# Gate weights by one rounded matmul per token, and all first products before the second ones

## What is computed

```python
idx = jnp.take_along_axis(cand_idx, pos, axis=-1)
g = jax.nn.softmax(top_s, axis=-1).astype(h.dtype)
...
def block(args):
    xt, it, gt = args
    u = expert_u[it]
    act = jax.nn.gelu(jnp.einsum('td,tkd->tk', xt, u))
    return jnp.einsum('tk,tkd->td', gt * act, expert_v[it])
```

## Time and profile before

| | us |
|---|---|
| median of three runs | 1509.1 (1508.21 to 1510.73) |
| the profiled execution, its time | 1509.89 |
| its span, first to last instruction | 1508.1 |
| TensorE busy | 1470.0 |
| VectorE busy | 889.2 |
| ScalarE busy | 819.0 |
| GpSimd busy | 576.4 |

### The profile page before, as it was taken

How to read it: one execution, slowest core, us unless ns; L and a number is a source line. 1 busy time by engine, 2 the same in 40 slices (tenths; PEclk the granted TensorE clock), 3 DMA queues, 4 the chain that set the end, 5 groups by cost and what they waited for, 6 DMA issues and landing times.

```text
span 1508.1 us, 24377 instructions
## 1 busy us (share of the span) xinstructions
PE 1470.0 (97%) x8923; PEld 1302.1 (86%) x8923; DVE 889.2 (59%) x2185; ACT 819.0 (54%) x1483; POOL 576.4 (38%) x200
## 2 busy tenths in 40 slices
PE   7999999999999999989999999999999999999998
PEld 6788888788889898889999998888888888887886
DVE  4935259388336431225996662666666666667776
ACT  5556454488456644443556664555555555555554
POOL 6881665700467477456888884000000000000000
PEclk9999999999999999999999999999999999999999
DMA  8740435600334335333665334555555555556774
GB/s 332 274 169 29 167 129 177 225 30 2 108 121 163 140 141 183 121 143 113 197 211 153 98 105 161 196 195 194 185 185 189 193 195 195 186 189 219 243 241 163
DMA packets 60125, 251.08 MB, mean 166 GB/s; under 512 B 6144, under 2 KB 18560, under 8 KB 44160
## 3 DMA queue, kind: packets, MB, share of 16 engines
q1 hardware_dynamic: 60032, 249.86, 47.9%
HBM read 242.50 MB, written 7.34 MB: 166 GB/s over the span
## 4 chain that ended last, share of the span: by engine, by line
PE 66%; POOL 2%; ACT 2%; DVE 1%; issue 1%; DMA 0%; DVEq 0%; ACTq 0%
PE bank L1297 23%; PE bank L1321 9%; PE bank L702 6%; PE bank L869 6%; PE bank L1324 5%; PE bank L1250 4%; PE bank L705 3%; POOL wlo L1364 2%; PE bank L822 2%; PE bank L764 1%; PE bank L805 1%; ACT whi L1421 1%; PE bank L724 1%; PE bank L998 1%; PE bank L1150 1%; PE bank L980 1%
## 5 line engine op out<-in xcount | busy, mean ns | idle before, releaser
L1364 POOL TENSOR_TENSOR wlo<-raw,whi 128x2048 fp32r<-128x2048 f32 (+1 forms) x51 | 195.3, 3840 | 159.0 <-ACT whi L1421 158.7
L1364 POOL TENSOR_TENSOR wlo<-arena,whi 128x2048 fp32r<-128x2048 f32 (+1 forms) x45 | 195.1, 4342 | 151.1 <-ACT whi L1421 150.9
L1297 PE MATMUL bank<-whi,ghi 128*128 128x512 f32 x512 | 201.4, 393 | 3.6 <-DVE glo L2559 1.7
L1297 PE MATMUL bank<-wlo,ghi 128*128 128x512 f32 x512 | 201.0, 393 | 0.0
L1297 PE MATMUL bank<-whi,glo 128*128 128x512 f32 x512 | 200.0, 391 | 0.0
L1321 PE MATMUL bank<-hT,whi 128*128 128x512 f32 x624 | 154.3, 390 | 1.6 <-ACT whi L1767 1.6
L1321 PEld LDWEIGHTS bank<-hT,whi 128*128 128x128 f32 x624 | 117.0, 188 | 26.0 <-ACT whi L1767 1.8
L2516 DVE TENSOR_TENSOR wlo<-raw,whi 128x1024 fp32r<-128x1024 f32 x84 | 102.8, 1225 | 56.6 <-ACT whi L1774 56.6
L1377 POOL TENSOR_TENSOR wlo<-raw,whi 128x1024 fp32r<-128x1024 f32 x52 | 123.8, 2391 | 28.2 <-ACT whi L1717 28.1
L1421 ACT ACTIVATE whi<-arena 128x2048 fp32r<-128x2048 f32 x41 | 78.4, 1915 | 94.4 <-PE bank L822 28.7
L822 PE MATMUL bank<-whi,hT 128*128 128x512 f32 x512 | 125.8, 393 | 0.0
(11 more groups left out here) (336 smaller groups left out, 3027.0 us busy)
## 6 DMA issues: line engine op xcount, KB each, us to landing
raw<-ex_in SPq DMA_DIRECT2D x52, 1024.0 KB, 4.8
raw<-w_in SPq DMA_DIRECT2D x44, 1024.0 KB, 5.2
arena<-w_in SPq DMA_DIRECT2D x44, 1024.0 KB, 5.1
raw<-ex_in SPq DMA_DIRECT2D x84, 512.0 KB, 3.9
xw<-ex_in SPq DMA_DIRECT2D x26, 1024.0 KB, 4.7
xw<-ex_in SPq DMA_DIRECT2D x16, 512.0 KB, 4.0
arena<-spill SPq DMA_DIRECT2D x48, 128.0 KB, 3.8
spill<-gact SPq DMA_DIRECT2D x32, 128.0 KB, 3.7
```

Of the source, the lines that this page charges most:

```text
L1297: last = mm(bank[2 * t + h][:, :], g[:, j % 2, tok], w[:, b, at], start=False, stop=(final and i == 2), skip_group_check=True)
L1364: last = G.tensor_tensor(wlo[:, u % 2, at], slots[u % RING][:, at], whi[:, u % 2, at], ALU.subtract)
```

## The change

All 128 first products are now taken in one stage, tiles 0 to 127, and all activations go to DRAM; then come all 128 second products, like the tail before. A *unit* is the `expert_u` half of a tile (n below 128) or the `expert_v` half (n from 128): `unit_hi`, `unit_lo`. Tiles 31 to 127 are merged.

W is built from tile 31 on: in each round of three tiles (n = 31 + 3g) one group g of eight tokens, in four *quarters* of two tokens, two behind the round's first tile and two behind its second. The gate values are themselves split in a rounded value and a remainder. One matmul of rounded operands with 256 columns gives a token's product with the rounded gate values and with their remainders (`hot_quarter`). ScalarE copies the one half to W, VectorE adds the other (`add_low`). For a group VectorE makes `plain` (1024 elements), from which GpSimd multiplies with the rounded gates (twice 512) and VectorE with the remainders (twice 512), and VectorE compares for the other side (twice 512; these four are `hots`). `iota8` is now read from SBUF. From tile 34 on every third remainder of the first products is made on VectorE.

In the second stage the activation m is read back (`load_act`) behind the load of unit m + 129.

```diff
+MERGED = 31
 GROUPS_W = T // 8
...
+NU = 2 * N_KEYS
+RING_OF = [n % 4 if n < G0 - 5 else n % 3 for n in range(NU)]
+LAST_OF_FOUR = max(n for n in range(NU) if RING_OF[n] == 3)
+BY_DVE = [n >= 2 * N_KEYS - 128 or (n > HOT0 and n % 3 == HOT0 % 3) for n in range(NU)]
...
+def quarters_at(i):
+    g, at = divmod(i - HOT0, 3)
+    return range(4 * g + 2 * at, 4 * g + 2 * at + 2) if 0 <= g < GROUPS_W and at < 2 else range(0)
...
+        plain_hot = quarters[3].rearrange("p (j n) -> p j n", j=8)
+        gated = [w[3].rearrange("p (a j n) -> p a j n", a=2, j=4) for w in (hi4, lo4)]
+        second_hot = [w[:, :, :].rearrange("p a t -> p (a t)").rearrange("p (j n) -> p j n", j=4) for w in (ghi, glo)]
+        staged = [gact[:, 0], gact[:, 1], xw[:, 4 * T:5 * T]]
+        again = [xw[:, T * (5 + i):T * (6 + i)] for i in range(3)]
...
+            def load_act(m):
+                if m >= 3:
+                    sp_.wait_ge(g_ready, m - 2)
+                sp_.wait_ge(act_stored[m % 3], 16 * (m // 3 + 1))
+                sp_.dma_start(again[m % 3], spill[m]).then_inc(act_back[m % 3], 16)
...
+                    by_dve, by_pool = lows_upto(earlier(n))
+                    if BY_DVE[earlier(n)]:
+                        sp_.wait_ge(u_lo_dve, by_dve)
+                    else:
+                        sp_.wait_ge(u_lo_pool, by_pool)
+                sp_.dma_start(quarters[RING_OF[n]], ex_d[n][:, 0:D] if n < N_KEYS else ex_d[n - N_KEYS][:, D:2 * D])\
+                   .then_inc(u_loaded[RING_OF[n]], 16)
+                if 6 <= n < N_KEYS + 6:
+                    store_act(n - 6)
+                m = n - 1 - N_KEYS
+                if m >= 0:
+                    load_act(m)
+            load_act(N_KEYS - 1)
...
+            def first_product(i):
+                h, l = (w[RING_OF[i]].rearrange("p (k n) -> p k n", k=KT) for w in (hi4, lo4))
+                else:
+                    pe.wait_ge(act_ready, i - 1)
+                if i == G0:
+                pe.wait_ge(u_hi, i + 1)
+                both = first_bank(i)[:, :].rearrange("p (s t) -> p s t", s=2)
+                out = both[:, 0 if i < MERGED else 1]
+                for k in range(KT):
+                    if i >= MERGED:
+                        mm(both, h[:, k, :], hT2[:, :, k, :], start=(k == 0), stop=False)
+                    for r, rows_of_k in enumerate((hThi, hTlo) if i < MERGED else ()):
+                        mm(out, h[:, k, :], rows_of_k[:, k, :], start=(k == 0 and r == 0), stop=False)
+                low_ready(i)
+                for k in range(KT):
+                    last = mm(out, l[:, k, :], hThi[:, k, :], start=False, stop=(k == KT - 1))
+                last.then_inc(u_done, 1)
+            def hot_quarter(k):
+                g, q = divmod(k, 4)
+                pe.wait_ge(hi_gated, g + 1)
+                pe.wait_ge(hots_ready, g + 1)
+                if k >= 2:
+                    pe.wait_ge(w_added, k - 1)
+                for j in range(2):
+                    token = 2 * q + j
+                    last = mm(hot_bank[k % 2][:, T * j:T * j + T].rearrange("p (a n) -> p a n", a=2),
+                              second_hot[token // 4][:, token % 4, :], gated[token // 4][:, :, token % 4, :], start=True, stop=True)
+                last.then_inc(w_done, 1)
...
+            for n in range(N_KEYS):
+                if not BY_DVE[n]:
+                    pool.wait_ge(u_hi, n + 1)
+                    G.tensor_tensor(lo4[RING_OF[n]], quarters[RING_OF[n]], hi4[RING_OF[n]], ALU.subtract).then_inc(u_lo_pool, 1)
+                g, at = divmod(n - HOT0 + 1, 3)
+                if at == 0 and 0 <= g < GROUPS_W:
+                    pool.wait_ge(plain_ready, g + 1)
+                    for half in range(2):
+                        some = slice(4 * half, 4 * half + 4)
+                        last = G.tensor_tensor(gated[half][:, 0], plain_hot[:, some],
+                                               idx8[:, 2, g, some].unsqueeze(2).to_broadcast([P, 4, P]), ALU.mult)
+                    last.then_inc(hi_gated, 1)
...
+            for n in range(NU - 2):
+                act.wait_ge(u_done, n + 1)
+                if n < N_KEYS:
+                    if n >= 3:
+                        act.wait_ge(act_stored[n % 3], 16 * (n // 3))
+                    if n >= MERGED:
+                        A(staged[n % 3], first_bank(n)[:, T:2 * T], ACT.Copy).then_inc(b_taken, 1)
+                    else:
+                        gelu(n)
+                    for k in quarters_at(n):
+                        act.wait_ge(w_done, k + 1)
+                        A(W[:, :, 2 * k:2 * k + 2].rearrange("p n t -> p t n"),
+                          hot_bank[k % 2][:, :].rearrange("p (t a n) -> p t a n", t=2, a=2)[:, :, 0, :],
+                          ACT.Copy).then_inc(w_copied, 1)
+                if n + 2 >= N_KEYS:
+                    act_hi(n + 2 - N_KEYS)
+                for j in next_in(n):
+                    unit_hi(j)
+                if MERGED <= n < N_KEYS:
+                    act.wait_ge(sum_ready, n - MERGED + 1)
+                    gelu(n)
...
-            V.tensor_copy(iota_ps, tb("iota", KEEP, keep)).then_inc(iota_ready, 1)
-            iota8 = iota_ps.unsqueeze(1).to_broadcast([P, 8, P])
+            iota8 = tb("iota", KEEP, keep).unsqueeze(1).to_broadcast([P, 8, P])
...
+            def plain(g):
+                if g == 0:
+                    dve.wait_ge(u_lo_pool, lows_upto(LAST_OF_FOUR)[1])
+                    dve.wait_ge(u_done, LAST_OF_FOUR + 1)
+                else:
+                    dve.wait_ge(w_done, 4 * g)
+                V.tensor_tensor(plain_hot, iota8, idx8[:, 1, g].unsqueeze(2).to_broadcast([P, 8, P]),
+                                ALU.is_equal).then_inc(plain_ready, 1)
+            def hots(g):
+                dve.wait_ge(plain_ready, g + 1)
+                for half in range(2):
+                    some = slice(4 * half, 4 * half + 4)
+                    V.tensor_tensor(gated[half][:, 1], plain_hot[:, some],
+                                    gate_lo8[:, g, some].unsqueeze(2).to_broadcast([P, 4, P]), ALU.mult)
+                    last = V.tensor_tensor(second_hot[half], iota8[:, 0:4],
+                                           idx8[:, 0, g, some].unsqueeze(2).to_broadcast([P, 4, P]), ALU.is_equal)
+                last.then_inc(hots_ready, 1)
+            def add_low(k):
+                dve.wait_ge(w_copied, k + 1)
+                to = W[:, :, 2 * k:2 * k + 2].rearrange("p n t -> p t n")
+                V.tensor_tensor(to, hot_bank[k % 2][:, :].rearrange("p (t a n) -> p t a n", t=2, a=2)[:, :, 1, :], to,
+                                ALU.add).then_inc(w_added, 1)
+            def weigh(m):
+                if m < N_KEYS:
+                    dve.wait_ge(act_back[m % 3], 16 * (m // 3 + 1))
+                    V.tensor_tensor(W[:, m, :], again[m % 3], W[:, m, :], ALU.mult).then_inc(g_ready, 1)
+            def act_lo(m):
+                if m < N_KEYS:
+                    dve.wait_ge(ghi_ready, m + 1)
+                    V.tensor_tensor(glo[:, m % 2, :], W[:, m, :], ghi[:, m % 2, :], ALU.subtract).then_inc(glo_ready, 1)
+            plain(0)
+            hots(0)
+            for n in range(HOT0 - 3, NU - 2):
+                some = quarters_at(n)
+                if MERGED <= n < N_KEYS:
+                    dve.wait_ge(b_taken, n - MERGED + 1)
+                    first = first_bank(n)[:, 0:T]
+                    V.tensor_tensor(first, first, staged[n % 3], ALU.add).then_inc(sum_ready, 1)
+                if len(some) and some[0] % 4 == 2 and some[0] // 4 + 1 < GROUPS_W:
+                    plain(some[0] // 4 + 1)
+                for k in some:
+                    add_low(k)
+                if len(some) and some[0] % 4 == 2 and some[0] // 4 + 1 < GROUPS_W:
+                    hots(some[0] // 4 + 1)
+                if n == N_KEYS - 2:
+                    dve.wait_ge(w_added, 4 * GROUPS_W)
+                    weigh(0)
+                if n + 2 >= N_KEYS:
+                    act_lo(n + 2 - N_KEYS)
+                if n + 3 >= N_KEYS and n + 3 - N_KEYS >= 1:
+                    weigh(n + 3 - N_KEYS)
+                if n + 3 < NU and BY_DVE[n + 3]:
+                    unit_lo(n + 3)
```

More of the change, by code:

```diff
@@ L29, with earlier, next_in, lows_upto @@
 PH = 8
[L30 to L37, removed]
+EXP_AT = (12, 23)
+SEL_AT = (19, 27)
 G0 = 29
+HOT0 = 31
+MERGED = 31
 GROUPS_W = T // 8
[L40 to L55, removed]
+NU = 2 * N_KEYS
+RING_OF = [n % 4 if n < G0 - 5 else n % 3 for n in range(NU)]
+LAST_OF_FOUR = max(n for n in range(NU) if RING_OF[n] == 3)
+BY_DVE = [n >= 2 * N_KEYS - 128 or (n > HOT0 and n % 3 == HOT0 % 3) for n in range(NU)]
+def earlier(n):
+    same = [j for j in range(n) if RING_OF[j] == RING_OF[n]]
+    return same[-1] if same else None
+def next_in(n):
+    return [j for j in range(n + 1, min(n + 5, NU)) if earlier(j) == n]
+def lows_upto(n):
+    return sum(BY_DVE[:n + 1]), n + 1 - sum(BY_DVE[:n + 1])
```

(24 more changed lines are left out.)

405 lines of the change are left out of this document (67 added, 338 removed).

## The result

The changed kernel takes 1748.66 us as a median of 4 runs (1747.33 to 1756.97), the kernel before 1509.91 us on the same chip (4 runs, 1508.21 to 1513.26). The ratio is 1.159, 95% interval 1.1547 to 1.1632: 16% slower. I had forecast 1721 with a range of 1600 to 1750. The profiled execution took 1749.79 us with a span of 1748.0, so the sum to hold against the forecast's 1720 is 1748.

What follows compares the result with a forecast made beforehand. TensorE, 97% busy, bounded the kernel before; after the change VectorE and GpSimd's turns would make it wait. Start 822 + rounds 498 + 21 + second products 355 + 24 = 1720 us span, 1721 as median; range 1600 to 1750.

Steps and rivals of the forecast that it cites:

- TensorE's side: TensorE's work with all else hidden: weights 28.3 us shorter, merged tiles 2.1 shorter, seams gone; end at 1469 us.
- The start: First products: the first *plain* that counts starts at about 822 us, after 32 tiles from 724, quarters, product, copy and sum.
- The rounds: First products: VectorE and GpSimd alternate on SBUF, so a three-tile round takes 16.6 us, not 9.3; 30 rounds 498 us.
- the hand-over from *sum* to product B': In each round, *sum* of tile C and gelu with hand-overs, before product B' can start: 0.9 us.
- The clock: Holes of 5 us bring a half-speed TensorE stretch each round, 2.8 us of it on the path: +1.4 us a round.
- From the last *plain* to the second products: From the last round's start at 1320 to the end of product 127: 21 us for three products, quarters and clock.
- The second products: Last stage: 355 us at TensorE's pace, plus 24 (18 to 30) for reads queued behind loads that wait for lows.
- Stores: Activation stores on SyncE in the first products: hidden, costing nothing, but binding if the turns are otherwise.
- no exclusion: Rival: VectorE and GpSimd do not exclude each other; stores bind at 10.75 us a round, 1540 us; chance 0.12.
- Turns kept by VectorE: Rival: the four hots run as one piece; 13.2 us a round through the stores, 1613 us; chance 0.25.
- The clock stays: Rival: TensorE keeps full speed in the first products; rounds of 15.2 us, 1677 us; chance 0.15.
- all is hidden: Rival: no exclusion and sooner-landing DMAs leave TensorE's pace everywhere, 1469 to 1480 us, faster; chance 0.05.

Runs made afterwards that it cites:

- Experiment 9: Changed kernel with comparison list and gate remainders in PSUM, stores ahead of loads in SyncE's list, and activation reads one load earlier: 1484.89 us, ratio 0.9824 to the kernel before.
- (1): Changed kernel with GpSimd's two lows and two gate multiplications of each group moved to VectorE: 1628.78 us, ratio 1.0797 to the kernel before.
- experiment 2: Changed kernel with the list 0 to 127 and the gates' remainders in PSUM (fourth output bank): 1554.22 us, ratio 1.0289 to the kernel before.
- experiment 3: Changed kernel with only the list 0 to 127 in PSUM, the gates' remainders left in SBUF: 1631.05 us, ratio 1.0807 to the kernel before.
- Experiment 4: Kernel before, with its comparisons for the weights reading the list 0 to 127 from SBUF instead of PSUM: 1560.26 us, ratio 1.0333.
- experiment 5: Changed kernel with twenty spare 512-column products on TensorE ahead of its wait for the hots: 1684.42 us, ratio 1.1152 to the kernel before.
- experiment 6: Changed kernel with the read of a spilled activation one load earlier in SyncE's list: 1716.39 us, ratio 1.1354 to the kernel before.
- 8: Changed kernel with only the store put ahead of the load in SyncE's list: 1749.36 us, ratio 1.1584 to the kernel before.
- 7: Experiment 2 with the store also put ahead of the load in SyncE's list: 1517.63 us, ratio 1.0052 to the kernel before.

## Why the prediction was right, step by step

The forecast of 1721 came out 28 us low, and its range ends 1.3 us above the median of 1748.66; one of the four runs lies outside it. As spans, the start is 1.6 us late, the rounds are 13.5 longer, the stretch to the second products 1.2 and the second products 11.7. The mechanism of each step held. That the rounds came so close is in part luck: two errors in them have opposite signs.

**TensorE's side.** The forecast had the change saving TensorE 39 us, were all else hidden, with an end at 1469 us. Experiment 9 has a span of 1484.2, 24 below before's 1508.1. The second products take 355.1 us there, as forecast. The rest is at 1129.1 in place of 1114: 30 rounds of 9.61 instead of 9.3 are 9 us of the 15, and the first counted *plain* is 3 later (825.2 for 822).

**The start.** 822 was forecast, 823.6 measured in the changed kernel.

**The rounds.** Forecast 16.6, measured 17.05; 498 and 511.5 us. The mechanism is shown by four kernels: more work on VectorE alone made it faster (1), one operand of each moved to PSUM took the waits away (2), the waits came back exactly on the operations with two SBUF operands (3), and in the kernel before the same operand cost 50 us (4). The parts: *plain* and *hots* 10.5 forecast, 9.93 measured; the hand-over from *sum* to product B' 0.9, 1.17; product B' 2.97 + 1.4 = 4.37, 5.18; copy and *sum* 0.75, 0.76. The order differed: I had a *hot* between the two gate multiplications, but VectorE was then still busy with two *add_low* (1011.98, 1.42 us). That alone changes nothing in the sum, since the same instructions follow one another either way. The 0.6 us lies in the hand-overs: a low and the *hot* behind it take 2.79 and 2.74 us (from 1014.65 to 1017.44 and to 1020.18) where I had put 2.37 + 0.60, and the two gate multiplications with their *hot* 2.51 (from 1012.14) in place of 2.70. Experiment 4 shows the same overlap of records at each hand-over.

**The clock.** This is the term that was mis-sized. The forecast had 1.4 us a round at half speed; experiment 5 gives back 2.28. Product B' takes 5.18 us until its copy starts and 3.10 with the hole filled (1014.21 to 1017.31). The longer hand-over is the clock, too: 1.17 us here and 0.89 there, since the quarters in it take 1.19 us for four matmuls, and 0.71 there. I had taken the length of the slow stretch, 3.75 us, from the one behind a hole of 1.73 us in the earlier trace rows, and 0.9 of it under the quarters. It does begin under the quarters, at 1020.96, but lasts some 5.7 us, to the last two matmuls of product B'. Product and hand-over are 1.1 us a round above their terms together, or 32 us over 30 rounds; the shorter *hots* (0.57) take 17 back. That leaves 15, against the 13.5 by which the rounds were off; my steps add up to 16.52 and had been rounded to 16.6, which is the rest.

**From the last *plain* to the second products.** 21 forecast, 22.2 measured.

**The second products.** 355 + 24 forecast, 390.7 measured: +36. The mechanism (the read behind the load behind the low, three instead of four tiles ahead) holds by experiment 6, which takes exactly the 35.6 away. The size lies above my 18 to 30. It is the upper end without the 4 us of lead that I subtracted (126 x 0.27 = 34): the tile took 3.0 us, as with the landing of 4.0 that I had called an estimate. The median landing was 3.9. The stage at TensorE's own pace, 355, was right to 0.1 us (its terms, 344 and 11.8, add up to 355.8).

**Stores.** I had them hidden in the changed kernel and binding if the turns went. Both are shown, by 8 and 7. The rival "no exclusion" with stores binding was put at 10.75 a round and 1540; experiment 2, which is that case made real, has 10.54 and a span of 1547.4 (the profiled execution is the fastest of its four). With the sum's own second products (379 forecast, 389.9 there) the two agree to a few us.

**The rivals.** Turns kept by VectorE is out: VectorE's second and third *hot* each wait for a whole low. The clock stays was 1677; experiment 5, which makes it so, has a span of 1680.3, though with rounds of 14.77 for 15.2 and second products of 391 for 379. That all is hidden needed no exclusion and shorter landings, I had said. Beside the operands it needed a shorter path to the issue instead, and two changes in SyncE's list gave that (the reads' median landing is still 3.9 in experiment 9).

**A reading.** For the subtraction at 463.61 I gave 4.6 us and 4.7 as the cost of the same two pieces; the wait in it is then 0.8 or 0.9. Nothing in the sum hangs on it.

Of the 239 us lost, 194 go with the operands (experiment 5 puts the clock's part at 64), 37 with the stores' place and 33 with the reads'. Together they return 264, which is 25 more than was lost.

## What to carry to other kernels

Where two engines take turns at SBUF, as VectorE and GpSimd do here, look at the operands of each instruction before its duration: a comparison of 1.2 us with one operand in PSUM was free beside GpSimd, and with both in SBUF it cost up to 3.4 us inside its own record, where no view of idle time shows it. Compare instructions of one shape: a spread of 0.68, 1.42 and 2.86 us is a wait. Hidden work gets its price when the cover goes: the store's place in the queue was worth nothing with the turns and 37 us without, so repair the largest wait first and then measure the small ones again. And take TensorE's floor from starting times in an undisturbed stretch, not from a sum of busy time.

## What the runs showed of the hardware that I had not expected

The helper engine was a loss: with GpSimd idle the kernel was 120 us faster than with two lows and two multiplications of each round on it. The hand-over itself costs nothing: in experiment 4 a tile took 9.70 us where the durations sum to 10.6. TensorE's clock came back while the engine worked on: behind a hole of 4.85 us the mean was 0.52 from 1021 to 1027, a slow stretch of some 5.7 us, longer than the 3.75 us behind the 1.73 us hole in the earlier trace rows, and the quarter at 1026.94 took 0.64 us, its full speed, with no idle time in between. The length of a hole does not tell by itself whether a slow stretch follows: behind 1.73 us in the earlier trace rows and 2.10 us in experiment 3 it did, behind 1.62 us in the earlier trace rows and 1.73 us in each tile of experiment 4 it did not.
